# Gate rows over all 128 rows and an earlier place for the column forms in a matrix-memory mixer

## The chip, the cores and the metric

One core of a Trainium2 chip runs the whole program in one launch. Times are device microseconds of that core. TensorE (PE) multiplies, its weight loads are shown apart (PEld); VectorE (DVE), ScalarE (ACT) and GpSimd (POOL) work beside it, and SyncE (SP) issues the weight transfers.

## The reference, cut to what matters

The program is two blocks on 256 tokens of width 1024: a block of two layers (feed-forward, gated linear attention, feed-forward, then feed-forward, differential attention, feed-forward), and a second block of one layer with a mixer and a feed-forward. The change lies in that mixer. It works on 256 context tokens and 256 latent tokens and joins two things: a windowed attention of 8 heads, and a bidirectional matrix memory (mLSTM) of 4 heads. The memory in one direction, per head:

```python
b = jnp.cumsum(fc)                                   # running sum of log forget gates
d = jnp.where(lower, b[:, None] - b[None, :] + ic[None, :], -inf)
m_t = jnp.maximum(a_inter, d.max(-1))                # stabiliser
w_intra = jnp.exp(d - m_t[:, None])
s = (q @ k.T) * w_intra
h = (s @ v) / jnp.maximum(abs(s.sum(-1)), jnp.exp(-m_t))
```

The kernel does it without chunks: for each head and direction the weight of query i and key j is exp(g_j - M_i), masked, where g is the input gate less the running sum, and M the running maximum of g. So each (head, direction) needs one row over the 512 keys (g), laid on all 128 partitions, and for each query a number in a column (M and the running sum).

## The kernel before, in words

Every product is in fp32 by two halves (hi and lo, type fp32r): weights are loaded in units of 128x2048 into a ring of three, ScalarE rounds a unit to w_hi (`split_hi`, L171) and VectorE takes the rest as w_lo (`split_lo`, L177); a product is then three passes. The order on each engine is written out by hand; semaphores tie the engines.

The mixer's stage on PE (`mix_tensor`) goes as follows. Projections of keys, gates and queries; transposes of keys and queries (L2375, L2382); then `value_tile(0)` (24 products of 256 columns); `score_pair(0)` (L2393, scores of attention heads 0 and 1, 64 rows); the column forms (L2532: sixteen records of products with 8 rows and 4 columns that turn running sums and maxima into columns, copied by ScalarE for `columns`). Then the loop over 8 attention heads: transposes of the exponentials (L2542), the next score pair, the next value tile, and for each pair `att_values` (L2418, L2425). The scores of a pair need VectorE's copy of the turned queries (L2200) and ScalarE's copy of the turned keys (L1951); VectorE takes the maxima (`logits`, L2209), ScalarE the exponentials (L1958).

Inside head 6 of that loop and behind it come the memory's heads. `broadcast(h, t)` makes, for query tile t and each direction d, a 128x512 bank from two products: L2439 lays the gate row of head h on all partitions (weights: a column of `ml_pick`, repeated 128 times; moving: `ml_rows`), and L2441 adds the mask over 256 or 128 columns. `ml_rows` is the memory of another tile (`act_lo`), of which VectorE's `rows()` fills rows 0 to 7 and 64 to 71 with the high halves of the forward and backward g and rows 32 to 39 and 96 to 103 with the low halves. L2439 uses rows 0 to 39 for the forward direction, rows 64 to 103 for the backward one. ScalarE makes the exponentials from the bank (`weights`, L1989); only then may the bank be written again. VectorE multiplies with the memory's scores (`weigh`, L2261, from `ml_scores`, L2453, 64 rows), divides and joins the directions (`combine`, L2270 to L2279). PE turns the result (`ml_turn`, L2462) and multiplies with the values (`ml_values`, L2474). Between these PE has pieces of an output gate's projection (`first_gate_part`, L2494). Then the output projection (L224) and the border to the last feed-forward, where ScalarE squares the sums (L2102).

Of the kernel before, what the change touches and what calls it, by code (L numbers as in the profile page):

```python
# [7 lines left out]
F32R = mybir.dt.float32r  # L8
U8 = mybir.dt.uint8
ALU = mybir.AluOpType  # L10
# [3 lines left out]
P = 128  # L14
# [20 lines left out]
MH, MDK, MDV = 4, 64, 128  # L35
# [23 lines left out]
def build_blocks(nc, A, C, out, stages=ALL_STAGES, scratch=None):  # L59
# [13 lines left out]
    with ctx:  # L73
        def sb(name, shape, dt=F32):
            return ctx.enter_context(nc.sbuf_tensor(name, shape, dt))
# [3 lines left out]
        def sem(name):  # L79
            if name not in sems:  # L80
                sems[name] = ctx.enter_context(nc.semaphore(name))
            return sems[name]
# [12 lines left out]
        ident = sb("ident", [P, P])  # L95
# [10 lines left out]
        gate_row = sb("gate_row", [P, 2, D])  # L106
        ada_col = sb("ada_col", [P, 3, 2, KT])
        st = sb("st", [P, 192])
        ml_pick = sb("ml_pick", [P, MH], F32R)
        arena_cols = 18736  # L110
        arena = sb("arena", [P, arena_cols])

# [18 lines left out]
        acc_bank = [acc[:, n // 2, (n % 2) * 512:(n % 2) * 512 + 512] for n in range(4)]  # L131
# [72 lines left out]
        def natural_columns(pe, u, outs, tok, h_wait=None, n_cols=UC):  # L204

            pe.wait_ge(sem("unit_split"), u + 1)
            hi, lo = as_columns(w_hi, u), as_columns(w_lo, u)
            for t, o in enumerate(outs):
                r = slice(tok + t * P, tok + (t + 1) * P)
                for k in range(KT):  # L210
                    if h_wait is not None and k % 2 == 0:
                        pe.wait_ge(sem("h_ready"), h_wait + t * KT + k + 2)
                    last = product(pe, o, (h_hi[:, k, r], h_lo[:, k, r]),
                                   (hi[:, k, 0:n_cols], lo[:, k, 0:n_cols]), k == 0, k == KT - 1)
            return last
# [1527 lines left out]
        ml_rows = act_lo[:, :, :].rearrange("p a b -> p (a b)")  # L1743
# [6 lines left out]
        def att_head(n):  # L1750

            return n // 2 + ATG * (n % 2)
# [19 lines left out]
        def chained(eng, name, ins):  # L1772

            chain_count[name] = chain_count.get(name, 0) + 1
            ins.then_inc(sem("chain_" + name), 1)
            eng.wait_ge(sem("chain_" + name), chain_count[name])
# [8 lines left out]
        def copied(what):  # L1785
            return MIX_COPIES.index(what) + 1
# [350 lines left out]
        def mix_vector(eng, name):  # L2137
# [33 lines left out]
            def rows():  # L2171

                eng.tensor_copy(ml_rows[g8, :], forward).then_inc(sem("ml_rows_ready"), 1)
                eng.tensor_copy(ml_rows[g64, :], backward).then_inc(sem("ml_rows_ready"), 1)
                eng.wait_ge(sem("ml_rows_ready"), 2)
                eng.tensor_tensor(ml_rows[32:40, :], forward, ml_rows[g8, :].bitcast(F32), ALU.subtract)\
                    .then_inc(sem("ml_rows_ready"), 1)
                eng.tensor_tensor(ml_rows[96:104, :], backward, ml_rows[g64, :].bitcast(F32), ALU.subtract)\
                    .then_inc(sem("ml_rows_ready"), 1)
                one, two = st[:, 176:176 + MH], st[:, 180:180 + MH]  # L2180
                eng.tensor_tensor(one, ident[:, 0:MH], ident[:, 32:32 + MH], ALU.add)
                chained(eng, "ml", eng.tensor_tensor(two, ident[:, 64 + MH:64 + 2 * MH], ident[:, 96 + MH:96 + 2 * MH],
                                                     ALU.add))
                eng.tensor_tensor(ml_pick[:, :], one, two, ALU.add).then_inc(sem("ml_rows_ready"), 1)

            def convolve(n, o, src):

# [165 lines left out]
        def mix_tensor(pe, name):  # L2353
# [31 lines left out]
            def score_pair(n):  # L2385

                if n >= 2:
                    pe.wait_ge(sem("att_maxed"), 2 * n)
                for t in range(TT):
                    for h in (n, n + 1):  # L2390
                        g, b = att_head(h) // ATG, att_head(h) % ATG
                        r = slice(g * AHD, (g + 1) * AHD)
                        pe.matmul(acc_bank[2 * (h % 2) + t], att_qt[r, b, t * P:(t + 1) * P], att_kt[r, :], start=True,  # L2393
                                  stop=True).then_inc(sem("att_scores"), 1)

            def value_tile(n):

                if n == 0:
                    pe.wait_ge(sem("mix_copied"), copied("gate_i"))
                elif n % 2 == 0:  # L2400
                    pe.wait_ge(sem("mix_copied"), copied(f"mv{n // 2 - 1}"))
                last = natural_columns(pe, u + MIX_MV + n // 4, [bank[3][:, (n % 2) * UC:(n % 2 + 1) * UC]], (n % 4) * P)
                if n % 4 == 3:
                    last.then_inc(sem("unit_used"), 1)
                elif n % 4 == 1:
                    last.then_inc(sem("ml_pair"), 1)
# [22 lines left out]
            def broadcast(h, t):  # L2429

                for d in range(2):
                    if (h, t) == (0, 0):
                        pe.wait_ge(sem("att_maxed"), 2 * (AH - 2) + d + 1)
                        pe.wait_ge(sem("ml_rows_ready"), 5)
                        pe.wait_ge(sem("ml_masks"), 2)
                    else:
                        pe.wait_ge(sem("ml_exps"), 4 * h + 2 * t + d - 1)
                    r = slice(64 * d, 64 * d + 40)
                    pe.matmul(acc_bank[d], ml_pick[r, h:h + 1].broadcast_to([40, P]), ml_rows[r, :], start=True,  # L2439
                              stop=False)  # L2440
                    pe.matmul(acc_bank[d][:, ml_masked[d][t]], ml_ident, ml_blocks[:, ml_mask[d][t]], start=False,  # L2441
                              stop=True).then_inc(sem("ml_bcast"), 1)

            def ml_scores(h):
                r = slice((h % 2) * MDK, (h % 2 + 1) * MDK)
                if h == 0:
                    pe.wait_ge(sem("ml_qk_ready"), 2)
                for t in range(TT):
                    if h == 0:
                        pe.wait_ge(sem("att_maxed"), 2 * (AH - 1) + t + 1)  # L2450
                    else:
                        pe.wait_ge(sem("ml_weighted"), 4 * (h - 1) + 2 * t + 2)
                    pe.matmul(acc_bank[2 + t], ml_q[r, h // 2, t * P:(t + 1) * P], ml_k[r, h // 2, :], start=True,  # L2453
                              stop=True).then_inc(sem("ml_scores"), 1)
# [64 lines left out]
                ready(n)  # L2519
                add_rows(pe, u + N_MIX_IN + n, tiles(n), n == 0)  # L2520

            value_tile(0)
            pe.wait_ge(sem("att_k_ready"), 1)
            pe.wait_ge(sem("att_q_ready"), 2)
            pe.wait_ge(sem("mix_copied"), copied("mq"))
            score_pair(0)
            pe.wait_ge(sem("ml_g_ready"), 4)
            pe.wait_ge(sem("mix_copied"), copied("mk1"))
            for n, (tile_, first, row) in enumerate(((ml_ff, S, 0), (ml_f, S, MH), (ml_i, S, 0), (ml_i, 0, MH))):
                for t in range(TT):  # L2530
                    at = (2 * n + t) * MH
                    last = pe.matmul(bank[2][:, at:at + MH], tile_[0:8, first + t * P:first + (t + 1) * P],  # L2532
                                     ident[0:8, row:row + MH], start=True, stop=True)
            last.then_inc(sem("ml_fcol"), 1)
            for h in range(AH):
                pe.wait_ge(sem("att_exps"), 2 * h + 2)
                if h >= 1:
                    pe.wait_ge(sem("att_pt0_ready"), h)
                    pe.wait_ge(sem("att_pt1_ready"), h)
                for t in range(TT):  # L2540
                    for k in range(4):
                        last = pe.transpose(bank[t][:, k * P:(k + 1) * P], att_e[:, h % 2, t, k * P:(k + 1) * P],  # L2542
                                            ident[:, :])
                last.then_inc(sem("att_e_transposed"), 1)
                if h == AH - 2:
                    broadcast(0, 0)
                elif h == AH - 1:
                    ml_scores(0)
                elif h % 2:
                    score_pair(h + 1)  # L2550
                if h < AH - 1:
                    value_tile(h + 1)
                if h % 2:
                    att_values(h // 2)
            broadcast(0, 1)
            first_gate_part(0)
            first_gate_part(1)
            broadcast(1, 0)
            ml_scores(1)
            first_gate_part(2)  # L2560
# [421 lines left out]
```

## Time and profile before

| | us |
|---|---|
| median of 3 runs | 1393.77 (1389.6 to 1393.89) |
| the profiled execution | 1387.45 |
| its span, first to last instruction | 1385.6 |
| PE busy | 1359.6 |
| DVE busy | 971.3 |
| ACT busy | 725.3 |
| mean granted clock of TensorE | 0.994 |

Busy times are modelled for PE: a product that waits for the array to empty counts as busy. The mixer's stage takes about a tenth of the span; its chain of waits runs through PE for nearly all of it.

### The profile page before, as it was taken

How to read it: one execution, taken by the hardware profiler on the slowest of the kernel's cores; microseconds unless marked ns; L12 is line 12 of the kernel's file. 1: busy time of each engine (PE TensorE's matmuls, PEld its weight loads, DVE VectorE, ACT ScalarE, POOL GpSimd, SP SyncE). 2: the span in 40 equal slices, each digit the busy share in tenths (PEclk: the TensorE clock that was granted, in tenths of full speed). 3: DMA queues.
4: the chain of work that ended last, by engine and by line, in shares of the span. 5: the costliest groups of instructions: out<-in, count | busy, mean ns of one | idle time of the engine just before them, and what ended most of it. 6: DMA issues, size and time to landing. Idle time of an engine off the chain costs nothing.

```text
span 1385.6 us, 19422 instructions
## 1 busy us (share of the span) xinstructions
PE 1359.6 (98%) x7989; PEld 1185.8 (86%) x7989; DVE 971.3 (70%) x1134; ACT 725.3 (52%) x978; POOL 116.5 (8%) x173
## 2 busy tenths in 40 slices
PE   8999999999999999999999999999999999999998
PEld 7888889878888889888899878888888868888887
DVE  6788876966687777777776857566576775765564
ACT  6444457445544445444465755544455455644443
POOL 2100000200000000000023012000014002100000
PEclk9999999999999999999999999999999999999999
DMA  9877545424877647887555326554543212365551
GB/s 293 295 246 254 202 141 184 145 91 148 307 245 244 227 166 252 272 276 256 193 180 183 125 92 230 189 201 159 196 124 126 57 33 92 120 214 185 199 193 61
DMA packets 171959, 256.16 MB, mean 185 GB/s; under 512 B 4884, under 2 KB 145471, under 8 KB 168671
## 3 DMA queue, kind: packets, MB, share of 16 engines
q1 hardware_dynamic: 169534, 248.63, 53.2%
q0 software_dynamic: 2176, 6.24, 1.8%
q8 instruction: 63, 1.03, 0.3%
q14 instruction: 26, 0.21, 0.0%
q10 hardware_dynamic: 160, 0.05, 0.0%
HBM read 253.59 MB, written 1.32 MB: 184 GB/s over the span
## 4 chain that ended last, share of the span: by engine, by line
PE 58%; DVE 3%; ACT 2%; issue 1%; POOL 0%; DVEq 0%; POOLq 0%; ACTq 0%
PE acc L224 15%; PE banks L615 15%; PE banks L625 8%; PE banks L186 3%; PE banks L187 3%; PE banks L188 3%; PE banks L575 2%; PE banks L605 1%; DVE w_lo L177 1%; PE banks L2474 1%; ACT w_hi L171 1%; PE acc L2393 1%; PE banks L2418 1%; DVE arena L313 1%; PE banks L2542 0%
## 5 line engine op out<-in xcount | busy, mean ns | idle before, releaser
L177 DVE TENSOR_TENSOR w_lo<-w_raw,w_hi 128x2048 fp32r<-128x2048 f32 x212 | 486.9, 2298 | 130.3 <-ACT w_hi L171 129.5
L171 ACT ACTIVATE w_hi<-w_raw 128x2048 fp32r<-128x2048 f32 x212 | 404.8, 1909 | 52.2 <-PE acc L224 17.2
L615 PE MATMUL banks<-h_both,w_hi 128*128 128x512 f32 x1520 | 371.2, 391 | 1.3 <-issue 1.3
L615 PEld LDWEIGHTS banks<-h_both,w_hi 128*128 128x128 f32 x1520 | 278.7, 188 | 55.5 <-issue 3.0
L625 PEld LDWEIGHTS banks<-h_both,w_lo 128*128 128x128 f32 x1520 | 194.9, 191 | 7.4
L625 PE MATMUL banks<-h_both,w_lo 128*128 128x256 f32 x1520 | 197.2, 283 | 0.0
L224 PE MATMUL acc<-w_lo,act_hi 128*128 128x512 f32 x400 | 155.9, 390 | 0.0
L224 PE MATMUL acc<-w_hi,act_hi 128*128 128x512 f32 x400 | 155.8, 390 | 0.0
L224 PE MATMUL acc<-w_hi,act_lo 128*128 128x512 f32 x400 | 155.8, 390 | 0.0
L471 ACT ACTIVATE silu_gate<-banks 128x512 f32<-128x512 f32 x55 | 32.9, 598 | 150.9 <-PE banks L615 133.8
L485 ACT ACTIVATE act_hi<-act 128x512 fp32r<-128x512 f32 x50 | 31.5, 630 | 138.7 <-PE acc L224 138.7
L224 PE MATMUL acc<-w_hi,h_both 128*128 128x512 f32 x272 | 90.3, 400 | 1.4 <-DVE h_both L947 1.2
L224 PEld LDWEIGHTS acc<-w_lo,act_hi 128*128 128x128 f32 x400 | 75.1, 188 | 16.0
L224 PEld LDWEIGHTS acc<-w_hi,act_hi 128*128 128x128 f32 x400 | 75.1, 188 | 15.8
L224 PEld LDWEIGHTS acc<-w_hi,act_lo 128*128 128x128 f32 x400 | 75.1, 188 | 15.7
L186 PE MATMUL banks<-w_hi,h_both 128*128 128x256 f32 x296 | 86.6, 293 | 0.9 <-DVE h_both L310 0.4
L187 PE MATMUL banks<-w_lo,h_both 128*128 128x256 f32 x296 | 84.3, 285 | 0.0
L188 PE MATMUL banks<-w_hi,h_both 128*128 128x256 f32 x296 | 84.3, 285 | 0.0
L480 ACT ACTIVATE act<-banks 128x512 f32<-128x512 f32 x50 | 29.9, 598 | 98.0 <-PE banks L615 98.0
L527 DVE TENSOR_TENSOR act_lo<-act,act_hi 128x512 fp32r<-128x512 f32 x50 | 34.5, 691 | 64.0 <-ACT act_hi L485 64.0
L512 DVE TENSOR_TENSOR act<-banks,act 128x512 f32<-128x512 f32 x50 | 34.5, 690 | 58.7 <-ACT act L480 58.7
L224 PEld LDWEIGHTS acc<-w_hi,h_both 128*128 128x128 f32 x272 | 51.9, 191 | 13.1 <-DVE h_both L947 1.4
(350 smaller groups left out, 1956.4 us busy)
## 6 DMA issues: line engine op xcount, KB each, us to landing
w_raw<-in_ffn_w_gu SPq DMA_DIRECT2D x88, 1024.0 KB, 5.2
w_raw<-in_ffn_w_down SPq DMA_DIRECT2D x44, 1024.0 KB, 4.8
arena<-in_w_ada SPq DMA_DIRECT2D x24, 1024.0 KB, 5.3
w_raw<-in_w_ffn_in SPq DMA_DIRECT2D x22, 1024.0 KB, 5.1
w_raw<-in_gla_w_in SPq DMA_DIRECT2D x12, 1024.0 KB, 5.2
w_raw<-in_diff_w_in SPq DMA_DIRECT2D x12, 1024.0 KB, 5.1
w_raw<-in_w_ffn_out SPq DMA_DIRECT2D x11, 1024.0 KB, 4.8
w_raw<-in_w_in SPq DMA_DIRECT2D x9, 1024.0 KB, 5.2
```

The lines of the kernel that those rows point to most:

```text
L171: eng.activation(w_hi[:, slot, :], w_raw[:, slot, :], ACT.Copy).then_inc(sem("unit_hi"), 1)
L177: eng.tensor_tensor(w_lo[:, slot, :], w_raw[:, slot, :], w_hi[:, slot, :].bitcast(F32), ALU.subtract).then_inc(sem("unit_split"), 1)
L186: pe.matmul(out_, a[0], b[0], start=first, stop=False)
L187: pe.matmul(out_, a[0], b[1], start=False, stop=False)
L188: return pe.matmul(out_, a[1], b[0], start=False, stop=last)
L224: mm = pe.matmul(acc[:, t, c], x[:, r], w[:, k, c], start=first and k + n == 0, stop=last and k + n == 3)
L471: eng.activation(silu_tiles, summands(GATE)[1], ACT.Copy).then_inc(sem("gate_low"), 1)
L485: eng.activation(act_pair(name, i)[0], act_tiles, ACT.Copy).then_inc(sem("act_hi_ready"), 1)
L512: eng.tensor_tensor(act_tiles, summands(UP)[0], act_tiles, ALU.add).then_inc(sem("up_summed"), 1)
L527: eng.tensor_tensor(lo, act_tiles, hi.bitcast(F32), ALU.subtract).then_inc(sem("act_lo_ready"), 1)
L615: return pe.matmul(outs[ct], hi[:, k, ct * P:(ct + 1) * P], h_both[:, k, :, t], start=k == 0, stop=k == KT - 1)
L625: pe.matmul(o[:, 0, :], lo[:, k, ct * P:(ct + 1) * P], h_hi[:, k, t], start=False, stop=False)
```

## The change

The gate rows' product now runs over all 128 rows of `ml_rows`. To that end `ml_pick` has one matrix for each direction, with ones at the two rows of head h of that direction and zeros everywhere else; the other rows of `ml_rows` are what the tile held before, and they are multiplied by zero. VectorE makes the two matrices by one addition each, from columns of the identity, without a sum in between. The column forms and the first score pair go ahead of value tile 0, in this order.

```diff
-        ml_pick = sb("ml_pick", [P, MH], F32R)
+        ml_pick = sb("ml_pick", [P, 2, MH], F32R)
...
-                one, two = st[:, 176:176 + MH], st[:, 180:180 + MH]
-                eng.tensor_tensor(one, ident[:, 0:MH], ident[:, 32:32 + MH], ALU.add)
-                chained(eng, "ml", eng.tensor_tensor(two, ident[:, 64 + MH:64 + 2 * MH], ident[:, 96 + MH:96 + 2 * MH],
-                                                     ALU.add))
-                eng.tensor_tensor(ml_pick[:, :], one, two, ALU.add).then_inc(sem("ml_rows_ready"), 1)
+                for d, at in ((0, 0), (1, 64 + MH)):
+                    eng.tensor_tensor(ml_pick[:, d, :], ident[:, at:at + MH], ident[:, at + 32:at + 32 + MH], ALU.add)\
+                        .then_inc(sem("ml_rows_ready"), 1)
...
-                        pe.wait_ge(sem("ml_rows_ready"), 5)
+                        pe.wait_ge(sem("ml_rows_ready"), 6)
...
-                    r = slice(64 * d, 64 * d + 40)
-                    pe.matmul(acc_bank[d], ml_pick[r, h:h + 1].broadcast_to([40, P]), ml_rows[r, :], start=True,
-                              stop=False)
+                    pe.matmul(acc_bank[d], ml_pick[:, d, h:h + 1].broadcast_to([P, P]), ml_rows, start=True, stop=False)
...
-            value_tile(0)
-            pe.wait_ge(sem("att_k_ready"), 1)
-            pe.wait_ge(sem("att_q_ready"), 2)
-            pe.wait_ge(sem("mix_copied"), copied("mq"))
-            score_pair(0)
             pe.wait_ge(sem("ml_g_ready"), 4)
             pe.wait_ge(sem("mix_copied"), copied("mk1"))
             for n, (tile_, first, row) in enumerate(((ml_ff, S, 0), (ml_f, S, MH), (ml_i, S, 0), (ml_i, 0, MH))):
...
             last.then_inc(sem("ml_fcol"), 1)
+            pe.wait_ge(sem("att_k_ready"), 1)
+            pe.wait_ge(sem("att_q_ready"), 2)
+            pe.wait_ge(sem("mix_copied"), copied("mq"))
+            score_pair(0)
+            value_tile(0)
             for h in range(AH):
```

## Rows read from the trace of the kernel before

**Rows 1.** The page: the span, and each engine's busy time, share and instructions.
```profile
span 1385.6 us, 19422 instructions
...
PE 1359.6 (98%) x7989; PEld 1185.8 (86%) x7989; DVE 971.3 (70%) x1134; ACT 725.3 (52%) x978; POOL 116.5 (8%) x173
```
**Rows 2.** Stretches: length, busy PE, PEld, DVE, ACT, POOL, granted clock, DMA share, GB/s.
```profile
225.00:229.00 4.00, 4.00 (x24) 4.00 (x23) 3.08 (x5) 3.97 (x5) 0.00 (x0) 0.57 0.00 0
...
1078.40:1081.90 3.50, 3.50 (x19) 3.50 (x18) 3.30 (x5) 1.21 (x4) 0.00 (x0) 0.51 0.25 19
...
1126.00:1150.10 24.10, 24.10 (x121) 16.14 (x119) 22.80 (x54) 14.58 (x27) 2.40 (x2) 1.00 0.13 45
1150.10:1153.60 3.50, 3.50 (x16) 3.13 (x16) 3.00 (x13) 1.29 (x2) 0.27 (x1) 0.51 0.81 269
```
**Rows 3.** Waits of PE, 1068 to 1168: us in total, times, longest.
```profile
PE banks L2542 <- ACT arena L1958: 0.7, 1, 0.7
PE banks L2418 <- ACT arena L2001: 0.2, 1, 0.2
```
**Rows 4.** Lines L2439 (durations in ns) and L2441 (idle before it, times).
```profile
L2439 PE MATMUL acc<-act_lo,ml_pick x16: 490/497/625, 1116.3 to 1149.9; 40*128 40x512 f32 x16
...
  issue: 4.5, 16
```
**Rows 5.** The chain that ended last: start, us, what (products merged).
```profile
1133.87 0.42 PE acc L2439
1134.29 0.26 PE acc L2441
1134.54 0.42 PE acc L2439
1134.96 0.32 PE acc L2441
1135.28 0.96 PE banks L2494 x8
...
1151.05 3.03 PE banks L2474 x16
...
1163.38 5.47 PE acc L224 x24
...
1169.28 1.79 PE banks L2474 x16
```
**Rows 6.** Timeline about the broadcasts: start, us, engine, line, what [idle before <-releaser].
```profile
1124.92 1.26 ACT L1989 ACTIVATE arena<-acc,st 128x512 f32<-128x512 f32 x2
...
1125.98 0.18 PEld L2439 LDWEIGHTS acc<-act_lo,ml_pick 40*128 40x128 f32 x1 [0.17 <-issue]
...
1136.04 0.69 DVE L2261 SCALAR_TENSOR_TENSOR arena<-acc,arena 128x512 f32<-128x512 f32 x1
...
1139.57 1.27 ACT L1989 ACTIVATE arena<-acc,st 128x512 f32<-128x512 f32 x2
1140.31 0.18 PEld L2439 LDWEIGHTS acc<-act_lo,ml_pick 40*128 40x128 f32 x1 [0.67 <-ACT arena L1989]
```
**Rows 7.** Timeline between the query transposes and those of attention head 0.
```profile
1068.63 0.34 DVE L2168 TENSOR_SCALAR arena<-arena 8x256 f32<-8x256 f32 x1
...
1069.94 0.19 PEld L186 LDWEIGHTS banks<-w_hi,h_both 128*128 128x128 f32 x1
...
1071.81 0.68 DVE L2200 COPY arena<-banks 128x512 f32<-128x512 f32 x1
...
1073.01 1.99 PE L2393 MATMUL acc<-arena 64*128 64x512 f32 x8
...
1074.92 1.94 PE L2532 MATMUL banks<-ident,arena 8*128 8x4 f32 x16
...
1077.59 0.86 PEld L2542 LDWEIGHTS banks<-ident,arena 128*128 128x128 f32 x8 [0.81 <-ACT arena L1958]
```
**Rows 8.** Timeline of PE about another fall of the clock, in an earlier stage.
```profile
220.85 3.72 PE L1130 MATMUL acc<-arena 32*128 32x256 f32 x16
```

## The prediction

> **What bounds the kernel now.** I read the page first: PE is busy for 98% of the span, the next engine, DVE, for 70% [rows 1]. So the question is what PE loses in the one stage that is changed, the mixer "mix". The table by stretches shows PE busy all of 1126 to 1150.1 at full clock, with DVE close behind (22.80 of 24.10 us), and two stretches of 3.5 us in which the granted clock is 0.51, the lower of its two levels [rows 2]. The list of waits holds two small ones of PE for ScalarE between 1068 and 1168, 0.7 and 0.2 us [rows 3]. By these views nothing else is to be had here; but a busy PE is not one at its peak. The view of the two lines of the broadcast shows it: all 16 mask products (L2441) come after an idle stretch of the weight loads that no semaphore explains, 4.5 us together [rows 4]. The chain of waits gives the true steps. One broadcast takes 0.42 + 0.26 + 0.42 + 0.32 = 1.42 us, while products whose operands have all 128 rows follow each other every 0.12 us at 256 columns (0.96 for 8), every 0.228 us at 512 (5.47 for 24) and every 0.11 us at 128 (1.79 for 16) [rows 5]. The reader is to see that the 40-row product costs nearly twice its 512 columns and that the mask products beside it are stretched too: going from 40 rows to 128 and back, the next load waits until the array is empty.
>
> The profiled execution took 1387.45 us, 1.85 more than its span; the median of the three timed runs lies 6.32 above it, at 1393.77. The sums are made on the profile and taken off the median.
>
> **Part 1: full-row products.** Sixteen products (4 heads, 2 tiles, 2 directions) go from 40 rows to 128. No row shows this product with 128 rows; its bounds are 0.228 us (the full-row product of 512 columns) and 0.42 (today's step). I take 0.228: operand types, columns and the weights' width are the same, only the rows differ. The mask products then go at 0.12 (256 columns) and 0.11 (128). A broadcast: 2 x 0.228 + 0.12 + 0.11 = 0.69 instead of 1.42, a gain of 0.73 at most. Broadcast by broadcast, named (head, tile):
> - (0,0) and (1,1) stand between full-row work: 0.73 each.
> - (0,1) comes after products with 64 weight columns; the 0.17 us ahead of its first load [rows 6] I leave in place: 0.55.
> - (1,0) and (3,0) are followed by 64-row score products, so the last mask product still drains (0.26 instead of 0.11): 0.58 each.
> - (2,0) must wait for the second exponential of (1,1). That one starts when the first mask product of (1,1) is done, which also comes earlier; by hand some 0.1 us of wait appears: 0.62.
> - (2,1) is held by ScalarE: its exponentials start at 1139.57 and take 1.27 for two, so the second bank comes free at 1140.84; today's first load is at 1140.31 [rows 6]. The second product could go 0.34 after the first and meets a wait of some 0.2; with the entry from 64 rows left as it is, 0.3.
> - (3,1) also enters from 64 rows: 0.5.
>
> Sum: 2 x 0.73 + 0.55 + 2 x 0.58 + 0.62 + 0.3 + 0.5 = 4.6 us. Bounds: nothing (0.42 stays) and 8 x 0.73 = 5.8.
>
> Does it reach the end? The chain runs through PE from here to the output projection, so what PE gives back, the rest of the stage does too, unless DVE becomes late. The closest meeting is the second score product of head 2, which needs the last weighing of head 1: DVE ends that at 1136.04 + 0.69 = 1136.73 and PE starts the product at about 1139.4, half of a 1.9 us pair ahead of the load at 1140.31 [rows 6]. The slack is 2.7 us, and PE will have won 0.73 + 0.55 + 0.58 + 0.73 + 0.62 = 3.2 by then. DVE itself begins this run of work 0.73 earlier, since it starts on PE's last attention product, behind broadcast (0,0); that makes 3.4. It just covers. If it didn't, the loss there would be 0.5.
>
> VectorE makes two picking columns directly instead of two halves and a sum: one addition and a wait less, two attention heads ahead of the first broadcast; PE's scores and value tiles hide it, and I give it nothing. The raised count (6 for 5) waits for the same place.
>
> A rule of the Trainium skill speaks against this part. The rows first: loads of 128 rows overlap the product in flight, or 24 products of 512 columns could not pass in 5.47 us [rows 5]. TensorE: Matmul & The Clock Gate, Part 3, The mechanism, has it that a weight load overlaps a running product only when the two use different row groups; full-row products use all of them. By that rule a product would cost load and stream one after the other, about what 40 rows cost now, and the part would bring nothing. The trace does not agree with it for full-row streams, so it keeps a small chance below.
>
> **Part 2: the new order.** Today: value tile 0 starts at 1069.94, scores at 1073.01, column forms at 1074.92 (1.94 us), then 0.7 us of wait for the first exponentials, transposes at 1077.59 [rows 3, 7]. After: the column forms start at 1069.94. Their wait on VectorE's last maximum (L2168) is over at 1068.63 + 0.34 = 1068.97, a slack of 1.0; everything on PE queues behind it if VectorE is later. They end at 1071.9. The scores need the second query copy, 1071.81 + 0.68 = 1072.49: PE stands for 0.6 us, since value tile 0 no longer covers that copy, and begins at 1072.55, 0.46 earlier than now. With 1.91 to the next load and 24 x 0.12 = 2.88 for the value tile, the transposes come at 1077.34. The exponentials, moved with the scores, are ready at 1077.13; PE is now the late one. Gain 0.25 us. No transfer is issued by what moves; VectorE's logits and the split behind them start 0.46 earlier and so does the next load of weights, with nothing in its way. Bounds: 0.73 of wait gone, if the copies came earlier, and a loss of as much if they came later.
>
> **The clock.** Its fall at 1078.40 follows 2.7 us in which PE had column forms of 8 rows and 4 columns and then the wait. The second fall, at 1150.1, follows products of 40 and 64 rows. That few rows are not enough is shown elsewhere: 16 products of 32 rows kept PE busy for 3.72 us from 220.85, and from 225 to 229 the clock was 0.57 [rows 2, 8]. A fall costs 3.5 x (1 - 0.51) = 1.7 us of full work; 16 products took 3.03 instead of 1.79, 1.24 more, and the broadcast at its start was slowed too [rows 5]. I take 1.5. With full rows in place of 40 the second fall may go; the timed runs differ by 4.3 us, so not every execution need have had it. I count half: 0.75. For the first I count nothing: the low stretch (column forms, then a wait) is as long as before, only 5 us earlier. Bounds for each: 1.5 either way.
>
> **Sum**: 4.6 + 0.25 + 0.75 = 5.6 us; the profile would show about 1382, the median 1388.2.
>
> **The rivals.**
> - Both falls go: 4.6 + 0.25 + 3.0 = 7.9, 1385.9. For it: value tile 0 now stands where the wait was. Against: 2.5 us of column forms and waiting remain.
> - VectorE paces the heads. In 1126 to 1150.1 it has 24.10 - 22.80 = 1.3 us of idle [rows 2]; if PE must wait for it, the stretch shrinks by 1.3, with 0.73 of (0,0) and 0.25 of the order 2.3: 1391.5. For it: the margin at head 2 is 0.2 us. Against: the other meetings have more.
> - The full-row form doesn't do it (loads don't overlap with this broadcast operand): 0.25, 1393.5. That is also where the skill's rule would end.
> - Slower: PE, now waiting for exponentials between broadcasts, has low stretches there, and the clock falls again and again. Each fall costs 1.5; from four more falls on it loses, 4 x 1.5 - 4.85 = 1.2: 1395. For it: the two falls that there are; against: clock 1.00 through all of 1126 to 1150.1 with the emptier 40-row products.
>
> **How the numbers follow.** Forecast 0.55, both falls gone 0.10, VectorE 0.20, no effect 0.09, slower 0.06. Runs scatter by some us, so the likeliest's own range is 1385.5 to 1391. The range of all, 1384.5 to 1393.5, leaves out the slower case and half of the one with no effect. About 0.3% (4.2 us) can be told from no change. The forecast is only 1.4 us beyond that bound, and I give a quarter of its chance to "same"; VectorE and no effect go there too. Faster 0.55, same 0.39, slower 0.06.
>
> **What would show it.** Right: L2439 with 128 rows at a step near 0.23 us, the idle before L2441 gone, broadcasts of 0.7 us in the chain; column forms at once behind the query transposes, some 0.6 us of PE's wait for VectorE's copy, none for the first exponentials; the squares behind the projection (L2102) some 5 us nearer to the query transposes. Wrong: steps of 0.4 with 128 rows; waits of PE for L2261 or L2279; clock falls inside 1120 to 1150.

## The result, and the profile after

| | before | after |
|---|---|---|
| median of 4 runs each, us | 1393.83 (1389.6 to 1394.23) | 1379.03 (1376.87 to 1381.42) |
| the profiled execution, us | 1387.45 | 1378.58 |
| its span, us | 1385.6 | 1376.8 |
| mean granted clock, profiled execution | 0.994 | 0.998 |

The ratio is 0.9896, with an interval of 0.9879 to 0.9913. The change gains 14.8 us where 5.6 were forecast; the time lies below the forecast's range. Most lines of the kernel after moved up by two to four: the transposes of the keys and, right behind them, of the queries are L2373 and L2380, the scores L2391, the column forms L2523, the transposes of the exponentials L2538, the broadcast L2436 and L2437.

The page of the kernel after: the span, and the engines' busy time, share and instructions.

```profile
span 1376.8 us, 19421 instructions
...
PE 1351.2 (98%) x7989; PEld 1181.3 (86%) x7989; DVE 970.9 (71%) x1133; ACT 724.9 (53%) x978; POOL 114.9 (8%) x173
```

PE is as full as in [rows 1], with as many products; it only needs 8.4 us less for them. The line L2436 of the kernel after, in the manner of [rows 4]:

```profile
L2436 PE MATMUL acc<-act_lo,ml_pick x16: 388/446/497, 1113.5 to 1142.7; 128*128 128x512 f32 x16
  ACT arena L1989: 1.7, 3
  issue: 0.2, 1
```

All 128 rows are in use, and the same view of the mask product (L2437) lists no idle stretch ahead of it, where there were 16. The chain of waits of the kernel after (start, us, what), beside [rows 5]:

```profile
1129.14 0.23 PE acc L2436
1129.37 0.06 PE acc L2437
1129.43 0.29 PE acc L2436
1129.72 0.12 PE acc L2437
1129.84 0.95 PE banks L2490 x8
...
1134.23 0.43 PE acc L2436
1134.66 0.06 PE acc L2437
1134.72 0.43 PE acc L2436
1135.15 0.11 PE acc L2437
```

The reader is to see a broadcast of 0.23 + 0.06 + 0.29 + 0.12 = 0.70 us where it was 1.42, and below it broadcast (2,1), 1.03, which ScalarE holds. The timeline of the kernel after, from the key transposes to those of head 0 (columns as in [rows 7]):

```profile
1067.68 0.46 PEld L2373 LDWEIGHTS acc<-ident,arena 128*128 128x128 f32 x4
...
1069.18 1.94 PE L2523 MATMUL banks<-ident,arena 8*128 8x4 f32 x16
1070.86 0.68 DVE L2198 COPY arena<-banks 128x512 f32<-128x512 f32 x1
1071.64 1.99 PE L2391 MATMUL acc<-arena 64*128 64x512 f32 x8 [0.52 <-issue]
...
1076.42 0.24 PEld L2538 LDWEIGHTS banks<-ident,arena 128*128 128x128 f32 x2
```

The column forms stand first, the scores wait 0.52 us until VectorE's copy has ended (1070.86 + 0.68 = 1071.54), and the transposes wait for nothing. The stretches of the kernel after (columns as in [rows 2]): an earlier stage, then from head 0 to the broadcasts, then the broadcasts and what follows.

```profile
225.00:229.00 4.00, 4.00 (x34) 3.83 (x33) 3.08 (x6) 3.96 (x5) 0.00 (x0) 1.00 0.00 2
...
1076.40:1113.50 37.10, 37.10 (x300) 30.26 (x298) 26.57 (x70) 20.32 (x48) 0.00 (x0) 1.00 0.14 31
...
1122.60:1143.60 21.00, 21.00 (x126) 15.86 (x124) 20.40 (x51) 14.62 (x28) 1.05 (x2) 1.00 0.14 51
1143.60:1172.00 28.40, 28.40 (x185) 25.64 (x184) 16.61 (x31) 15.77 (x31) 4.87 (x6) 1.00 0.35 110
```

All three falls of the clock in [rows 2] (0.57 at 225, 0.51 at 1078.4 and at 1150.1) are absent from this execution; one at 306, in an earlier stage, is in both (0.63 and 0.60 from 306 to 310). The account goes by three places: the first load of the key transposes (L2375, L2373), the first load of a broadcast, and the squares (L2102). Before:

```profile
1068.64 0.14 PEld L2375 LDWEIGHTS acc<-ident,arena 128*128 128x128 f32 x1
...
1116.29 0.18 PEld L2439 LDWEIGHTS acc<-act_lo,ml_pick 40*128 40x128 f32 x1 [0.17 <-issue]
...
1181.18 0.60 ACT L2102 ACTIVATE arena<-acc 128x512 f32<-128x512 f32 x1 [1.49 <-PE acc L224]
```

After:

```profile
1113.45 0.19 PEld L2436 LDWEIGHTS acc<-act_lo,ml_pick 128*128 128x128 f32 x1
...
1172.30 0.60 ACT L2102 ACTIVATE arena<-acc 128x512 f32<-128x512 f32 x1 [1.48 <-PE acc L224]
```

| stretch, profile against profile | before | after | gain | of which forecast |
|---|---|---|---|---|
| start to key transposes | 1068.64 | 1067.68 | 0.96 | 0 (the fall at 225) |
| to the transposes of head 0 | 8.95 | 8.74 | 0.21 | 0.25 |
| to the first broadcast | 38.70 | 37.03 | 1.67 | 0 (the fall at 1078) |
| to the squares | 64.89 | 58.85 | 6.04 | 4.6 + 0.75 |

That is 8.88 us from profile to profile. The rest of the 14.8 lies between the profiled executions and the medians: 6.4 before (1393.83 - 1387.45), 0.45 after. The experiments ask where those 6 us and the falls come from.

### The profile page after: what moved, and what is told of

It reads as the page before. It is cut to its first block, busy times and chain, and to the rows that moved or that the text cites. A ratio compares the mean times of both kernels' runs of the same rounds, so it can differ in the third digit from the quotient of the medians.

```text
span 1376.8 us, 19421 instructions
## 1 busy us (share of the span) xinstructions
PE 1351.2 (98%) x7989; PEld 1181.3 (86%) x7989; DVE 970.9 (71%) x1133; ACT 724.9 (53%) x978; POOL 114.9 (8%) x173
## 3 DMA queue, kind: packets, MB, share of 16 engines
q8 instruction: 63, 1.03, 0.3%
## 4 chain that ended last, share of the span: by engine, by line
PE 58%; DVE 3%; ACT 2%; issue 1%; POOL 0%; DVEq 0%; POOLq 0%; ACTq 0%
PE acc L224 16%; PE banks L615 15%; PE banks L625 8%; PE banks L186 3%; PE banks L188 3%; PE banks L187 3%; PE banks L575 2%; PE banks L605 1%; DVE w_lo L177 1%; ACT w_hi L171 1%; PE acc L2391 1%; PE banks L2416 1%; DVE arena L313 1%; PE banks L2470 1%; PE banks L2538 0%
```

## The experiments

In the texts on record, A1 is the theory that the full rows take away clock falls among the broadcasts, A2 that the new order does; H1 and H2 are explained where they come in. "This kernel" stands for the one run, "before" for the kernel before, run again beside it on the same chip.

**e1: the kernel before, once more, for an execution far above the profiled one.** No edit.

> The kernel before once more, for a second profile of it. Theory A (the clock): its timed runs at about 1394 us have more stretches at the lower clock in the mixer than the first profile (two there, two in earlier stages); at 1390 us or more this profile shows four or more such stretches between the query transposes and the output projection. Rival B (time lost elsewhere): the same four stretches in all, and a stage other than the mixer longer by some us.

Measured: 1394.26, and its profile shows what the first one did not. Windows of this execution of the kernel before:

```profile
1116.00:1132.10 16.10, 15.91 (x92) 10.53 (x91) 10.81 (x25) 10.13 (x14) 0.00 (x0) 1.00 0.19 66
1132.10:1152.60 20.50, 20.50 (x63) 14.40 (x63) 14.01 (x33) 5.93 (x9) 0.00 (x0) 0.50 0.15 52
```

And its chain of waits inside:

```profile
1134.22 0.72 PE acc L2439
1134.94 0.41 PE acc L2441
1135.35 0.72 PE acc L2439
1136.07 0.51 PE acc L2441
```

One fall of 20.5 us, granted clock 0.50, in the middle of the broadcasts, with PE never idle: a broadcast takes 2.36 us instead of 1.42. It was expected as several stretches and came as one. The 24 runs of the kernel before in this comparison fall into groups: 11 at 1384.5 to 1385.0, 2 at 1387.4 to 1387.6, one at 1389.6, ten at 1393.8 to 1394.8. Over this and the three later comparisons 48 of 105 runs lie at 1393.7 to 1394.9, with a mean granted clock of 0.989 or 0.990; the group about 1384.7 has 0.996 or 0.997. So the long fall costs 1394.4 - 1384.7 = 9.7 us, and the median of the kernel before is that of a mixture: 1387.5 to 1387.7 in three comparisons, 1393.89 in the fourth.

**e2: full rows alone**, in the old order (the two matrices of `ml_pick` come with them).

```diff
-                    pe.matmul(acc_bank[d], ml_pick[r, h:h + 1].broadcast_to([40, P]), ml_rows[r, :], start=True,
-                              stop=False)
+                    pe.matmul(acc_bank[d], ml_pick[:, d, h:h + 1].broadcast_to([P, P]), ml_rows, start=True, stop=False)
```

> Full-row products alone, the old order. Theory A1 (the 40-row products pull the clock down): the structural 4.6 us and most of the rest, 1380 to 1384 us. A2 (the column forms and the wait behind them pull it down): 4.6 us alone, about 1389. Both A: the broadcast stretch, first broadcast to output projection, 4.6 us shorter at equal clock.

Measured: 1380.17 (1378.58 to 1381.22, 7 runs), ratio 0.9923 [0.9895, 0.9951]. Windows of e2:

```profile
1078.20:1081.50 3.30, 3.30 (x17) 3.30 (x16) 3.23 (x5) 1.39 (x5) 0.00 (x0) 0.50 0.19 26
1115.00:1150.00 35.00, 34.81 (x235) 27.20 (x232) 28.77 (x65) 25.01 (x44) 1.89 (x4) 1.00 0.21 67
```

Without the new order the fall at 1078 stays; the broadcasts keep the full clock, and none of the 7 runs shows the long fall, beside 10 of 24 of the kernel before. A1's number fits; A2's, about 1389, does not. The stretch from the first broadcast to the squares takes 58.85 us, as in the kernel after.

**e3: the new order alone**, with the 40 rows.

```diff
-            value_tile(0)
...
-            score_pair(0)
...
             last.then_inc(sem("ml_fcol"), 1)
...
+            score_pair(0)
+            value_tile(0)
```

> New order alone, 40-row products kept. A1: about 1392 to 1393 us (0.25 us and one fall of the clock at most). A2: 1384 us or less. Transposes of attention head 0 come 0.2 us earlier after the query transposes than before.

Measured: 1383.26 (1381.35 to 1387.41, 12 runs), ratio 0.9964 [0.9942, 0.9986]; no run at 1390 or above. A1, which left the long fall in place here, fails; A2's number fits. So either part by itself goes without the long fall, and they don't add: 1380.2 and 1383.3 alone, 1379.0 together. The profile of e3 has the full clock from the key transposes to the squares, which makes it the measure for the rows:

```profile
1067.69 0.46 PEld L2375 LDWEIGHTS acc<-ident,arena 128*128 128x128 f32 x4
...
1176.94 0.60 ACT L2102 ACTIVATE arena<-acc 128x512 f32<-128x512 f32 x1 [1.49 <-PE acc L224]
```

That is 109.25 us, and 104.62 in the kernel after, which differs from e3 by the rows alone: 4.63.

**e4: 64 rows instead of 40**, old order.

```diff
-                    r = slice(64 * d, 64 * d + 40)
-                    pe.matmul(acc_bank[d], ml_pick[r, h:h + 1].broadcast_to([40, P]), ml_rows[r, :], start=True,
+                    r = slice(64 * d, 64 * d + 64)
+                    pe.matmul(acc_bank[d], ml_pick[r, h:h + 1].broadcast_to([64, P]), ml_rows[r, :], start=True,
```

> The kernel before with its gate rows laid by products of 64 rows in place of 40 (added rows have zero weights), old order; the drains between few-row and full-row products stay. If the number of rows in a product counts for the clock: some falls go, 1388 to 1392 us. If only the drains count, or full rows alone: 1393 to 1394, as before. Step of one broadcast 1.42 us in both.

Measured: 1385.86 (1383.45 to 1394.6, 12 runs), ratio 0.9994 [0.9965, 1.0022]; 4 of 12 at 1393.8 or above. The product with 64 rows, L2439 in e4:

```profile
L2439 PE MATMUL acc<-act_lo,ml_pick x16: 490/497/498, 1116.3 to 1149.9; 64*128 64x512 f32 x16
```

Its 497 ns are those of 40 rows in [rows 4], and its broadcasts take 1.42 us in the chain of waits: the step is unchanged. The long fall is there too, by the time and the mean granted clock (0.989 or 0.990) of the four runs; the profiled one, 1385.81, has none. Both ranges were missed, since they were set against 1393.8 and the kernel before lay at 1387.46 in this comparison.

**e5: the kernel after with its drains put back**: a 32-row product of 4 columns, overwritten at once, ahead of each full-row product.

```diff
+                    pe.matmul(acc_bank[d][:, 0:4], ml_pick[0:32, d, h:h + 1].broadcast_to([32, P]), ml_rows[0:32, 0:4], start=True,
+                              stop=True)
                     pe.matmul(acc_bank[d], ml_pick[:, d, h:h + 1].broadcast_to([P, P]), ml_rows, start=True, stop=False)
```

> The changed kernel with a product of 32 rows and 4 columns put ahead of each of the 16 full-row products (its columns are overwritten by that product), so that the array goes from full rows to few rows and back as before, with next to no work in it. If the drains are what the 40-row form costs: broadcasts of 0.63 to 0.70 us become 1.2 to 1.5, the kernel 4 to 6 us slower than the changed one, 1382 to 1385. If the 40-row products were slow by themselves and drains cheap: within 1.5 us of the changed kernel. Theory: few-row products pull the clock down only where they take up the time; full rows remain here, so no execution at 1390 or more.

Measured: 1383.55 (1381.69 to 1386.69, 12 runs), ratio 0.9965 [0.9946, 0.9984]; no run at 1390 or above. The chain of waits in e5, where L2436 is the 32-row product, L2438 the full-row one and L2439 the mask:

```profile
1131.19 0.20 PE acc L2436
1131.38 0.42 PE acc L2438
1131.81 0.06 PE acc L2439
1131.87 0.20 PE acc L2436
1132.06 0.42 PE acc L2438
1132.49 0.12 PE acc L2439
```

The very product that took 0.23 us takes 0.42 behind one of 32 rows, and the short one, 4 columns, takes 0.20 behind full rows. The broadcast is back at 1.42. From the key transposes to the squares e5 takes 109.74 us at full clock, 5.1 more than the kernel after (the medians, from two chips, differ by 4.5): the loss that part 1 meant to take away is back, with full rows in place. It lies in the passage from few rows to all and back, not in the 40 rows as such. The kernel before shows this too, in one place of its chain of waits: among the 64-row scores of head 3, with no full-row product ahead of it, the 40-row product takes 0.22 us of the chain. (It lies on other rows than the scores beside it, so overlap with them may be part of that.)

```profile
1147.81 0.62 PE acc L2453
1148.43 0.22 PE acc L2439
```

The Trainium skill has in TensorEngine Tiling (Array Packing), Key Properties, that a change of tiling mode drains TensorE. The traces agree and give a price: 0.19 us more for the full-row product behind few rows, and 0.20 for a product of 4 columns behind full rows, where the column forms follow each other every 0.12 (1.94 for 16). That no run came to 1390 says nothing of the clock, since the broadcasts of e5 lie where those of e3 do (46.0 us behind the key transposes).

**e6, e7: does the place decide?** Under H1 the long fall hangs on where the broadcasts lie behind the key and query transposes; under H2 it only follows upon a fall at 1078. Sixteen identity products go behind value tile 0, into e3 (e6) and into the kernel after (e7).

```diff
             value_tile(0)
+            keep_warm(pe, 16)
```

> New order alone (40 rows), with 16 transposes of the identity (16 x 0.11 = 1.8 us) behind value tile 0, which move everything behind them later by as much as the missing fall of the clock had. Theory H1 (the long fall comes back when the 40-row stretch lies where it lay before): a third or more of the executions at 1393 or above, the others at 1383 to 1388. H2 (the long fall needs the first fall, at the column forms): all executions at 1383 to 1389, 1.8 us above the new order alone.

> The changed kernel with the same 16 transposes. Theory (full rows keep the clock up wherever the stretch lies): 1.8 us above the changed kernel, 1378.5 to 1382, no execution above 1384. Rival (the changed kernel too was only well placed): some executions near 1390.

Measured: e6 1387.59 (1385.08 to 1389.77, 12 runs), ratio 0.9985 [0.9962, 1.0007]; e7 1382.57 (1380.3 to 1385.13, 12 runs), ratio 0.9953 [0.9933, 0.9973]. No long fall in either. But the filling took twice what was meant: each of these fp32 products is two records of 0.11 us, 16 of them 3.7 us instead of 1.8. So e6 went past the place it aimed at and decides nothing; nor does e7, with full rows at a place where 40 rows had no long fall either. Its median and its highest run, 1385.13, lie about 1 us above what was expected, with 1.9 us of filling more than meant.

**e8: the old order with the wait ahead of head 0 filled**, by six identity products behind the column forms.

```diff
             last.then_inc(sem("ml_fcol"), 1)
+            keep_warm(pe, 6)
```

> The kernel before (40 rows, old order) with 6 transposes of the identity in the wait behind the column forms, where PE stands 0.7 us. If few columns and the wait make the first fall: that fall is gone from the profile and the short executions come to 1383 to 1384.5. H1: long falls may stay or go, as with the new order alone, since what follows lies 1.5 us earlier. H2: no execution at 1390 or above, since there is no first fall.

Measured: 1384.77 (1381.98 to 1385.16, 12 runs), ratio 0.9956 [0.9934, 0.9978]. Windows of e8:

```profile
1072.00:1082.00 10.00, 10.00 (x78) 8.62 (x77) 7.91 (x18) 5.03 (x13) 0.00 (x0) 1.00 0.54 117
1082.00:1160.00 78.00, 77.81 (x540) 59.79 (x539) 55.01 (x139) 44.54 (x84) 3.90 (x4) 1.00 0.18 54
```

The fall at 1078 is gone, and the long one is in none of 12 runs. Both hypotheses allow that. The runs come in two groups, 1382.0 to 1382.4 and 1384.8 to 1385.2, on either side of the range of 1383 to 1384.5.

**e9, e10: a first fall forced**, by making the column forms three times, in e3 (e9) and in the kernel after (e10).

```diff
-            for n, (tile_, first, row) in enumerate(((ml_ff, S, 0), (ml_f, S, MH), (ml_i, S, 0), (ml_i, 0, MH))):
+            for n, (tile_, first, row) in 3 * list(enumerate(((ml_ff, S, 0), (ml_f, S, MH), (ml_i, S, 0), (ml_i, 0, MH)))):
```

> New order alone (40 rows), with the column forms made three times over: 32 more products of 8 rows and 4 columns, 3.7 us, of which 0.5 lie where PE waits for the query copy. This forces a low stretch and so a first fall of the clock, with the rest of the new order kept. H2 (the long fall in the 40-row stretch comes only behind a first fall): executions at 1395 or more come back, a quarter of them or more, beside others at 1386 to 1390. Rival (the place of the column forms, or something else in the old order, is what matters): a first fall in the profile, but all executions within 1385 to 1391.

> The same in the changed kernel (full rows). Theory: a first fall there too, all executions 3 to 5 us above the changed kernel, 1381 to 1386, no long fall, since full rows keep the clock up in the broadcast stretch after any fall.

Measured: e9 1389.87 (1386.11 to 1392.43, 12 runs), ratio 1.0005 [0.9985, 1.0025]; e10 1384.24 (1381.62 to 1387.81, 12 runs), ratio 0.9955 [0.9936, 0.9974]. Windows of e9:

```profile
1073.80:1080.60 6.80, 6.80 (x24) 4.25 (x24) 2.03 (x6) 0.37 (x1) 0.00 (x0) 0.50 0.39 83
1116.00:1160.00 44.00, 43.81 (x273) 31.75 (x272) 32.39 (x75) 28.20 (x51) 3.90 (x4) 1.00 0.21 72
```

A first fall of 6.8 us stands ahead of broadcasts with 40 rows, and none of 12 runs shows the long one: H2's forecast fails here, and e13 below, which has the long fall without a first, settles it. The highest run of e9, 1392.43, is also above what the rival allowed. e10 has the first fall too (0.50 from 1074 to 1078) and no long one, as forecast, but neither has e9 with 40 rows; its highest runs, 1387.7 and 1387.8, are above the range.

**e12, e13: the broadcasts put back to their old place.** e12 is e3 with eight identity products, 1.85 us, at the place of e6's sixteen; e13 is e8 with ten instead of six, which fills the wait, keeps the first fall away and ends where the kernel before does.

> New order alone (40 rows) with 8 products of the identity behind value tile 0. In the shift before this one each such product turned out as two records, so 16 of them took 3.7 us where 1.8 were meant; 8 take 1.85, and the 40-row stretch lies again where the kernel before has it after its first fall. H1 (place): 30% or more of the executions at 1393 or above. H2 is already without support. Neither: all at 1383 to 1389, and what the long fall needs beside few rows stays open.

> The kernel before with 10 products of the identity (2.3 us) behind the column forms: no first fall, and the 40-row stretch at the place where the first fall had put it (0.7 us of wait is covered, 1.6 us are added, for 1.5 of the fall). H1: 30% or more of the executions at 1393 or above. Neither: all at 1383 to 1388.

Measured: e12 1388.13 (1385.05 to 1397.15, 12 runs, 5 of them at 1393.8 or above), ratio 0.9989 [0.9966, 1.0011]; e13 1388.68 (1384.85 to 1394.71, 12 runs, 5 of them at 1393.8 or above), ratio 0.998 [0.9955, 1.0005]. Windows of e13:

```profile
1076.00:1116.00 40.00, 40.00 (x322) 32.99 (x321) 28.25 (x77) 22.10 (x53) 0.00 (x0) 1.00 0.15 34
1132.70:1153.10 20.40, 20.40 (x65) 14.34 (x64) 13.62 (x32) 6.44 (x9) 0.00 (x0) 0.50 0.15 51
```

The long fall is back with no first fall ahead of it. For e12 it is read from the times and the mean granted clock (0.989 to 0.991); the profiled execution, 1387.94, has none. From the first load of the key transposes to the first load of a broadcast, in the profiles:

| kernel | rows | us | runs with the long fall |
|---|---|---|---|
| before | 40 | 47.65, and 47.68 in e1 | 48 of 105 |
| e4 | 64 | 47.65 | 4 of 12 |
| e13 | 40 | 47.62 | 5 of 12 |
| e12 | 40 | 49.47, with a first fall worth 1.6 in it | 5 of 12 |
| e3 | 40 | 45.98 | 0 of 12 |
| e8 | 40 | 46.73 | 0 of 12 |
| e6 | 40 | 49.56 | 0 of 12 |
| e9 | 40 | 52.16 | 0 of 12 |
| e2 | 128 | 47.47 | 0 of 7 |
| e14 (below) | 128 | 47.38 | 0 of 4 |
| after | 128 | 45.77 | 0 of 4 |
| e5 | 128 | 46.00 | 0 of 12 |
| e7 | 128 | 49.36 | 0 of 12 |
| e10 | 128 | 51.93 | 0 of 12 |
| e11 (below) | 128 | 46.29 | 0 of 6 |

H1 fits, for the places tried: the long fall was met with 40 or 64 rows and broadcasts at about 47.7 us. A single microsecond less, e8, and 12 runs are without it. Two things are not shown. e12 lies at that place (47.8) only in an execution without its first fall; with it, it lies where e6 does, which had no long fall. No profile shows which of the two its five slow runs were, and two of them, at 1396.9 and 1397.2, are some 2.6 us above the other three. And that full rows are safe at that place rests on the 11 runs of e2 and e14, placed by one profile each; the other kernels with full rows lie where 40 rows had no long fall either. Why that place counts, and why the same program at it has the fall in some executions only, is not settled.

**e11, e14: can the kernel after be bettered?** A fall of its clock at 306 is left, behind two waits of PE at the end of the linear attention. e11 fills these with ten and nine identity products, puts four into the wait for the query copy, and moves one piece of the gate's projection ahead of broadcast (2,1); e14 has five and four products, the gate's piece and nothing else.

```diff
+                if t:
+                    for _ in range(5):
+                        pe.matmul(bank[0][:, P:2 * P], ident[:, :], ident[:, :], start=True, stop=True)
...
+            for _ in range(4):
+                pe.matmul(acc_bank[0][:, 0:P], ident[:, :], ident[:, :], start=True, stop=True)
...
+                    first_gate_part(4)
                     broadcast(2, 1)
-                    first_gate_part(4)
```

> The changed kernel with three additions that its profile points to: transposes of the identity in two waits of PE at the end of the linear attention, ahead of the clock's fall at 306 us (10 and 9 of 0.11 us in waits of 1.5 and 1.4), 4 in the wait for the query copy, and a piece of the output gate ahead of broadcast (2,1), where PE waits 0.4 us. If waiting alone makes the fall at 306, it goes: 1.5 to 1.7 us; the order gives 0.3. About 1.9 us below the changed kernel's executions without other falls, 1375 to 1377. If it stays, 0.3 us or a loss of up to 0.5.

> The candidate with half the filling (5 and 4 products of the identity, 1.1 and 0.9 us, in the two waits at the end of the linear attention) and none at the query copy; a piece of the output gate ahead of broadcast (2,1) as before. The fall at 306 us gone at no cost: 1.5 us, and 0.3 from the order; 1375 to 1377 where no other fall comes, 1377.5 in the middle. If the filling still delays the work behind it: as the changed kernel, 1379.

Measured: e11 1379.57 (1378.8 to 1381.31, 6 runs), ratio 0.9925 [0.9901, 0.9949]; e14 1378.48 (1376.58 to 1379.24, 4 runs), ratio 0.9892 [0.9867, 0.9917], beside 0.9896 of the kernel after. Windows of e14:

```profile
303.00:306.00 3.00, 2.79 (x26) 2.60 (x25) 1.60 (x5) 1.17 (x4) 0.00 (x0) 1.00 0.00 0
306.00:310.00 4.00, 3.71 (x19) 2.94 (x18) 2.40 (x7) 3.66 (x7) 0.00 (x0) 1.00 0.02 4
...
1071.70:1075.10 3.40, 3.40 (x12) 1.52 (x9) 1.75 (x6) 0.09 (x1) 0.00 (x0) 0.55 1.00 247
```

The fall at 306 is absent from both profiles, but also from that of e10, where that stage is as it was (granted clock 1.00 from 306 to 310); the other thirteen profiles have it. So the filling may have taken it away, and two profiles don't show it. Both forecasts were missed. In e11 the filling, again twice as long as meant, may have given the gain back by delaying what follows, which no run tests; e14 can't be told from the kernel after. Its profile has a fall behind the column forms, the last line above, though the order there is that of the kernel after. The gate's piece gave 0.13 us of the 0.3: from the first broadcast to the squares both take 58.72 instead of 58.85.

## Why the prediction was wrong, step by step

- **Full rows, 4.6 us: right as a sum.** The row of 0.228 us was the one to take: the step is 0.23 between full-row products, and e3 and the kernel after lie 4.63 apart. The parts came out less well, and that their errors cancel is luck. By the chains of waits of e3 and of the kernel after, (0,0) gave 0.78, (0,1) 0.54, (1,1) 0.71 and (2,1), held by ScalarE, 0.29, all near the forecast. (1,0) and (3,0) gave 0.77 and 0.78 for 0.58, since the last mask product stays short (0.06) ahead of 64-row scores; (2,0) gave 0.77 for 0.62, since the wait expected there did not come. But (3,1) with its scores gave 0.12 for 0.5, since with 40 rows one of its two products already stood among the scores at 0.24, and the 16 products behind it take 0.17 more than in e3.
- **No effect, the rival: no.** Full-row loads of 0.19 us lie beside products that follow each other every 0.23 us. The overlap that the Trainium skill, TensorE: Matmul & The Clock Gate, Part 3, The mechanism, ties to different row groups (it names a background weight buffer beside them) is there with the load and the product both on all 128 rows; the measurement decides.
- **VectorE as the pace: no.** From 1122.6 to 1143.6 it is busy for 20.40 of 21.00 us, as close as feared, but PE's list of waits from 1066 to 1160 in the kernel after has no line for it but the copy's:

```profile
PE acc L2391 <- issue: 0.5, 1, 0.5
PE banks L2416 <- ACT arena L2001: 0.2, 1, 0.2
```

- **The order, 0.25 us: right**, at 0.21, with 0.52 us of wait for the 0.6.
- **The clock, 0.75 us: this step failed**, and only in its size; it was worth about 10, the 14.8 less 4.6 and 0.2. Two terms make that up. From profile to profile it is 4.1: falls of 0.96 at 225, 1.48 at 1078 and 1.62 at 1150 (against e3, which has none of the three). The price of 1.5 was right, but the first of the two counted on was put at nothing because the low stretch "is as long as before", and it was absent; the one at 1150 was absent whole, not half; and the one at 225 lies ahead of all that was changed, so that its absence is luck. Without it the profiles differ by 7.9, which is the rival "both falls go", given a chance of 0.10. Whether the change took these falls away one execution doesn't show: e14, in the new order, has one behind the column forms, and e4, in the old order with 64 rows, has none at 1150. The other term is the 6 us between the profiled executions and the medians. The long fall costs 9.7 us in some half of the kernel before's executions, three of the four in the first comparison, and is in none of the changed kernel's. The prediction made its sums on the profile and took them off the median, so the 6.32 us between the two were carried over unchanged, as if they were scatter. They were mostly one event that this profile had missed.
- **"The clock falls again and again": the wrong side.** It was the kernel before that lost its clock there. The reason held against it, clock 1.00 from 1126 to 1150.1 with the emptier products, was itself luck: e1 has 0.50 from 1132.1 on.

How much of the 14.8 belongs to the change? At like clock, 0.996 or 0.997, the kernel before takes 1384.7 and the kernel after 1379.48 (one run): 5.2, where the two steps by hand give 4.85. The rest is clock, in the main the long fall. That belongs to the change too as far as either half of it, full rows (e2) or the new order (e3), goes without it at 0 of 7 and 0 of 12; but its share depends on how often the kernel before meets it, 9 of 23 runs on one chip and 15 of 23 on another.

## What to carry to other kernels

Ahead of a forecast, hold the timed runs against the profiled execution: where they lie in groups, or off it by more than the profile's own falls are worth, the profile has not shown the event that sets the median, and its mean granted clock beside that of the runs tells so at once. A product with few rows amid products with all rows costs two drains, 0.4 us here, and padding it with rows that are multiplied by zero cost nothing here. Short products that fill a wait should be sized from a row of their own kind before they are placed.

## What the runs showed of the hardware that was not expected

- PE that is never idle does not keep its clock: in e1 and e13 it was busy for all of 20.4 to 20.5 us at 0.50, while it ran 40-row broadcasts, 64-row scores and full-row pieces between them. With 128 rows at the same place, e2, the clock stayed at 1.00 in the profile, and none of 7 runs took more than 1381.22.
- The same program at the same place shows a long fall in some executions and none in others: times come in groups (1384.7, 1387.5, 1389.7, 1394.4), each with its own mean granted clock (0.996 to 0.997, 0.994, 0.993, 0.989 to 0.990), and hardly between them.
- A shift of a microsecond, worth nothing by itself, decided over 9.7: e8 and e13 differ by four identity products, and 0 of 12 runs against 5 of 12 have the long fall. They ran on two chips, but the kernel before had it on both, in 14 of 35 runs beside e8 and in 15 of 23 beside e13.
- An identity product in plain fp32 is two records. The timeline of e6 (columns as in [rows 7]) has 32 of them for its 16 products, in 3.73 us, 0.23 for a product:

```profile
1076.67 3.73 PE L376 MATMUL banks<-ident 128*128 128x128 f32 x32
```
